# A decoder layer on one core: the odd units of the expert weights issued by GpSimd instead of SyncE

## The chip, the core and the metric

The kernel runs on one NeuronCore of one Trainium2 chip, as one launch. The metric is the device time of the launch in microseconds (us). Of the kernel before, three runs are given with their median.

## The reference, cut to what matters

One step of one decoder layer for 256 prompt tokens and 8 sample tokens, all in float32, width 1024. Behind the attention parts stands a mixture of 32 experts:

```python
logits = xf @ w_router + b_router                 # 264 tokens, 32 experts
top_logit, top_idx = lax.top_k(logits, 4)
gates = jax.nn.softmax(top_logit, axis=-1)
...
gu = xblk @ w_gate_up[e] + b_gate_up[e]           # (1024, 2048) for each expert
g, u = jnp.split(gu, 2, axis=-1)
g = jnp.minimum(g, 7.0); u = jnp.clip(u, -7.0, 7.0)
act = (u + 1.0) * g * jax.nn.sigmoid(1.702 * g)
return act @ w_down[e] + b_down[e]                # (1024, 1024) for each expert
```

Each expert has 8 MB of gate and up weights and 4 MB of down weights (MB here is 1,048,576 bytes), so all 32 hold 384 MB, that is 402.7 million bytes. All of it is read once.

## The kernel before, in words

**Stages.** Projections, convolution, windowed attention, memory attention and the router come first. Their weights and cached keys and values stream through `ring`, 12 slots of 1 MB in SBUF. After that comes the expert stage, which is the longer part.

**Items, units and places.** The experts are taken in pairs (A, B), two pairs to a round, eight rounds. A pair is 24 items of 1 MB: 8 of gate and up for A, 8 for B, 4 of down for A, 4 for B (`item_of`, L523). Two neighbouring items are a unit of 2 MB, so a pair has 12 units, a round 24 (`ROUND // 2`), and all experts 192; this text numbers them 0 to 191. There is room for 16 items, which makes 8 places (`UNITS`), and unit u always goes to place u % 8. `PLACES` (L147) says where a place lies: places 1, 2, 3, 4, 6 and 7 are two neighbouring slots of the ring, place 0 is 16 KB per partition of other memory, and place 5 is two pieces of 8 KB per partition that do not lie side by side. A unit is therefore one DMA of 2 MB with 16 KB for each partition, but at place 5, an odd one, it is two DMAs of 1 MB with 8 KB for each partition (`unit_load`, L631). Place 5 holds units 5, 13, ..., 181, 189.

**Who issues.** All expert weights are issued by SyncE (SP), in order of u, on its one DMA queue. Before it issues unit u, `unit_read` (L648) makes SP wait until TensorE has read unit u - 8, which lay at the same place. The first 8 units are issued late in the attention stages, as the memory for them comes free; the other 16 units of round 0 follow one by one, and a loop (`round_loads`, L661) issues the seven further rounds. A second loop is there for inputs in which an expert has more tokens than 64 slots hold; it is behind an `If` and the profile shows no load of it.

**Who waits.** TensorE takes the items in order. `item_arrived` (L543) waits for the semaphore of the unit's place. `gate_up` (L2114) multiplies the tokens of one expert by 8 items; for A it also scatters the pair before (L2184) between items. `down` (L2156) multiplies by 4 items. Between them stand a turning of the activations (L2153) and the gathering of the next pair's tokens (L2098). The last pair also has L2205, sums that prepare the last layer norm. After the last unit come L2245, the layer norm and the stores of the outputs.

**GpSimd (POOL).** It issues small loads and stores over a queue of its own (the queue called software_dynamic in the profile) and computes little: two subtractions at L797 that the gathering waits for, and two operations on the output rows at the very end (L802, L804). Between L797 and L802 it has nothing to do.

Of the kernel before, what the change touches and what calls it, by code (L numbers as in the profile page):

```python
# [149 lines left out]
def decoder_layer(nc, x_prompt, x_sample, mem_prompt, cache_win_k, cache_win_v, state_conv, cache_mem_k,  # L150
# [4 lines left out]
    with ctx:  # L155
        def sem(name):
            return ctx.enter_context(nc.semaphore(name))
# [333 lines left out]
        def reader_done(eng, n):  # L491

            what, i = STREAM[n]
            if what == "xp":
                eng.wait_ge(s_xT, DC)
            elif what == "mp":
                eng.wait_ge(s_mT, DC)
            elif what == "win":
                piece_used(eng, 2 * i + 1)
            elif what == "wout" and i < 2:  # L500
                eng.wait_ge(s_sd, 1)
            elif what == "wmo" and i < 3:
                eng.wait_ge(s_sd, 2)
            elif what in GROUP0:
                if i % 2 == 0:
                    eng.wait_ge(s_half, GROUP0[what] + i // 2 + 1 - GROUP0["wmv"])
                else:
                    per = 2 if what in ("wmv", "wmk") else 4
                    eng.wait_ge(s_dn, TILE0[what] + per * (i // 2 + 1))
            elif what == "qb":  # L510
                eng.wait_ge(s_kq, 2 * i + 2)
            elif what == "wk":
                eng.wait_ge(s_kr, i + 1)
            elif what == "mqb":
# [66 lines left out]
        down_rows = w_down[0]  # L581
        pos = sample_positions()
        assert pos == list(range(0, 512, 16)) + list(range(512, 896, 4)) + list(range(896, PAST))

        block = ctx.enter_context(nc.Block())

# [3 lines left out]
        def _(sp):  # L590
# [40 lines left out]
            def unit_load(e0, u):  # L631

                k, i = item_of(2 * u)
                e = e0 + k
                if i < 8:
                    src = gate_rows[bass.ds(e, 1), i * P:(i + 2) * P, :].rearrange("a (p s) n -> p (a s) n", s=2)
                else:
                    src = down_rows[bass.ds(e, 1), (i - 8) * 2 * P:(i - 6) * 2 * P, :].rearrange(
                        "a (p s v) n -> p (a s) (v n)", s=2, v=2)
                w, done, first = u % UNITS, unit_landed(u), unit_first(u)  # L640
                if w and first is None:
                    for s in range(2):
                        sp.dma_start(expert_slot(2 * w + s), src[:, s, :]).then_inc(done, 16)
                else:
                    dst = ring[:, first:first + 2, :].rearrange("p a n -> p (a n)") if w else extra_whole
                    sp.dma_start(dst, src.rearrange("p s n -> p (s n)")).then_inc(done, 16)

            def unit_read(k0, u):  # L648

                k, i = item_of(2 * u + 1)  # L650
                k += k0
                if i < 7:
                    sp.wait_ge(e_wu, 7 * k + (i + 1))
                elif i == 7:
                    sp.wait_ge(e_gu, k + 1)
                elif i < 11:
                    sp.wait_ge(e_du, 3 * k + (i - 7))
                else:
                    sp.wait_ge(e_dn, k + 1)

            def round_loads(e0, before):  # L661

                for u in range(ROUND // 2):
                    if u < UNITS:
                        unit_read(before, u + ROUND // 2 - UNITS)
                    else:
                        unit_read(before + 4, u - UNITS)
                    unit_load(e0, u)


            sp.wait_ge(s_av, H + MH)
            sp.wait_ge(s_mst, 32)
            unit_load(0, 0)
            for u in range(1, UNITS):
                at = PLACES[u]
                if at is None:
                    sp.wait_ge(s_sat, 4)
                else:
                    reader_done(sp, NPRE + at - RING)
                    reader_done(sp, NPRE + at + 1 - RING)  # L680
                unit_load(0, u)
            for u in range(UNITS, ROUND // 2):
                unit_read(0, u - UNITS)
                unit_load(0, u)
            with sp.Fori(1, NX // 4) as r:
                round_loads(r * 4, (r - 1) * 4)

            sp.wait_ge(s_nsw, 4)
            rounds = sp.value_load(nswi[0:1, 1:2], min_val=8, max_val=40)
            with sp.If(rounds > NX // 4):  # L690
                with sp.Fori(NX // 4, rounds) as r:
                    round_loads((r % 8) * 4, (r - 1) * 4)
# [16 lines left out]
        def _(pool):  # L709
# [75 lines left out]

            pool.wait_ge(s_kvst, 96)
            pool.dma_start(wr, w_router[0].rearrange("(c p) e -> p c e", p=P)).then_inc(s_late, 16)
            pool.wait_ge(s_dn, 56)
            pool.dma_start(g3[:, 0, :], ln3_g.broadcast_to((P, D))).then_inc(s_g3, 16)
            pool.dma_start(g3[:, 1, :], ln3_b.broadcast_to((P, D))).then_inc(s_g3, 16)  # L790
# [4 lines left out]
            for t in range(2):  # L795
                pool.wait_ge(s_x2b, t + 1)
                nc.gpsimd.tensor_tensor(x3[:, t, 2, :], rest[:, t, :], x3[:, t, 1, :], ALU.subtract).then_inc(s_x3, 1)  # L797

            y1 = yo[:, LORDER[0], :]
            pool.wait_ge(s_g3, 32)  # L800
# [1475 lines left out]
```

## Time and profile before

| | |
|---|---|
| median of 3 runs | 1275.05 us (1274.89 to 1276.47) |
| the profiled execution | 1275.87 us |
| its span in the profile | 1274.1 us, granted TensorE clock 0.995 |
| TensorE busy | 1205.9 us, 95% of the span |
| VectorE, ScalarE, GpSimd busy | 373.0, 201.1, 39.0 us |
| DMA | 485.10 million bytes, mean 381 GB/s |

The span is the time from the first to the last instruction of the program; the profiled execution's own time is 1.77 us more, and lies 0.82 us above the median. A matmul's end is modelled in the profile, so that TensorE can show as busy without being at its peak. GB/s are 10^9 bytes a second.

### The profile page before, as it was taken

To read this page: it belongs to the slowest core of one execution; us is meant where nothing else is said; L and a number is where in the kernel's file an instruction comes from. 1 tells how busy PE (TensorE), PEld (TensorE's weight loads), DVE (VectorE), ACT (ScalarE), POOL (GpSimd) and SP (SyncE) were. 2 spreads that over 40 slices of the span, in tenths; PEclk is the share of its full clock that TensorE was granted. 3 is DMA by queue.
4 is the path that set the end of the run, shared out by engine and by line. 5 is a ranking of instruction groups with operands and counts; after the bars stand their busy time and mean duration, and the time that the engine had idled before them with its cause. 6 is when DMAs were issued, how large, how long until landed. Compare 5 with 4: busy or idle time off the path is not lost.

```text
span 1274.1 us, 16471 instructions
## 1 busy us (share of the span) xinstructions
PE 1205.9 (95%) x6600; PEld 569.8 (45%) x6600; DVE 373.0 (29%) x919; ACT 201.1 (16%) x328; POOL 39.0 (3%) x62
## 2 busy tenths in 40 slices
PE   7999999999999999999989999998989898989896
PEld 6995467876533434344333333232333333233332
DVE  4555735633530221302122021302021211202123
ACT  4443331222301101011010101010101101010101
POOL 2201000100100000000000000000000000000001
PEclk9999999999999999999999999999999999999998
DMA  9984896899499999999999999999999999999993
GB/s 331 292 252 137 264 348 254 333 366 393 165 399 426 429 427 427 428 426 430 426 427 427 427 429 427 427 427 427 426 429 426 428 427 426 430 427 426 426 425 160
DMA packets 62645, 485.10 MB, mean 381 GB/s; under 512 B 6192, under 2 KB 6532, under 8 KB 34352
## 3 DMA queue, kind: packets, MB, share of 16 engines
q1 hardware_dynamic: 58576, 469.36, 90.5%
q0 software_dynamic: 3872, 15.12, 3.7%
q8 instruction: 26, 0.43, 0.1%
q10 hardware_dynamic: 160, 0.10, 0.0%
q14 instruction: 11, 0.09, 0.0%
HBM read 479.40 MB, written 5.17 MB: 380 GB/s over the span
## 4 chain that ended last, share of the span: by engine, by line
PE 62%; DMA 33%; DVE 2%; ACT 1%; issue 1%; SPq 0%; POOL 0%; DVEq 0%; ACTq 0%; POOLq 0%
PE ps L2126 25%; DMA ring<-in_w_gate_up_dram 16%; DMA late<-in_w_gate_up_dram 13%; PE ps L1686 11%; PE ps L2166 6%; PE ps L2184 5%; PE ps L1723 5%; DMA late<-in_w_down_dram 3%; PE ps L2098 1%; PE ps L1867 1%; DMA arena<-in_b_gate_up_dram 1%; PE ps L2153 1%; DMA arena<-in_state_conv_dram 1%; PE ps L2192 1%; PE ps L1889 1%; PE ps L1666 1%
## 5 line engine op out<-in xcount | busy, mean ns | idle before, releaser
L2126 PE MATMUL ps<-ring,arena 128*64 128x512 f32 x1536 | 360.2, 600 | 13.8 <-DMA ring<-in_w_gate_up_dram 13.8
L1583 DVE TENSOR_TENSOR arena<-arena,ps 128x264 f32<-128x264 f32 x128 | 55.2, 431 | 574.7 <-PE ps L2184 574.7
L2126 PEld LDWEIGHTS ps<-ring,arena 128*64 128x64 f32 x1536 | 98.9, 136 | 199.1 <-issue 161.0
L2166 PE MATMUL ps<-ring,arena 128*64 128x512 f32 x768 | 171.6, 596 | 13.5 <-DMA ring<-in_w_down_dram 13.5
L2166 PEld LDWEIGHTS ps<-ring,arena 128*64 128x64 f32 x768 | 53.7, 137 | 118.1 <-issue 104.4
L1004 ACT ACTIVATE arena<-arena 128x512 f32<-128x512 f32 x32 | 20.2, 632 | 471.2 <-DVE arena L1566 471.2
L2184 PE MATMUL ps<-arena 128*128 128x264 f32 x256 | 91.2, 438 | 0.0
L2126 PE MATMUL ps<-late,arena 128*64 128x512 f32 x384 | 90.0, 596 | 0.0
L1686 PE MATMUL ps<-arena,ring 128*128 128x256 f32 x384 | 88.1, 380 | 0.0
L2184 PEld LDWEIGHTS ps<-arena 128*128 128x128 f32 x256 | 38.1, 188 | 103.8 <-issue 103.8
L1723 PE MATMUL ps<-x_split,w_split 128*128 128x264 f32 x384 | 73.7, 293 | 6.7 <-DVE ring_split L1037 6.7
L1686 PEld LDWEIGHTS ps<-arena,ring 128*128 128x128 f32 x384 | 70.8, 189 | 10.9 <-issue 1.8
L1723 PEld LDWEIGHTS ps<-x_split,w_split 128*128 128x128 f32 x384 | 61.6, 195 | 7.9 <-DVE ring_split L1037 7.8
L1686 PE MATMUL ps<-ring,arena 128*128 128x512 f32 x128 | 57.0, 593 | 0.0
L1723 PE MATMUL ps<-x_split,ring_split 128*128 128x264 f32 x192 | 55.8, 290 | 0.0
L2126 PE MATMUL ps<-arena 96*64 96x512 bf16 (+1 forms) x256 | 50.7, 495 | 4.5 <-DMA late<-in_w_gate_up_dram 3.7
L1566 DVE TENSOR_SCALAR arena<-ps 128x512 f32<-128x512 f32 x32 | 22.2, 692 | 111.8 <-PE ps L2126 111.3
L1006 ACT COPY arena<-ps 128x512 f32<-128x512 f32 x32 | 18.8, 587 | 221.1 <-PE ps L2153 221.1
L2098 PE MATMUL ps<-arena 128*128 128x128 bf16 x768 | 52.6, 219 | 1.1 <-issue 1.1
L2098 PEld LDWEIGHTS ps<-arena 128*128 128x128 bf16 x768 | 49.9, 98 | 2.1 <-issue 1.9
L2166 PE MATMUL ps<-late,arena 128*64 128x512 f32 x192 | 44.2, 595 | 6.2 <-DMA late<-in_w_down_dram 6.2
L2126 PEld LDWEIGHTS ps<-late,arena 128*64 128x64 f32 x384 | 25.8, 136 | 45.2 <-issue 42.2
(297 smaller groups left out, 954.7 us busy)
## 6 DMA issues: line engine op xcount, KB each, us to landing
ring<-in_w_gate_up_dram SPq DMA_DIRECT2D x96, 2048.0 KB, 33.8
ring<-in_w_down_dram SPq DMA_DIRECT2D x48, 2048.0 KB, 34.3
late<-in_w_gate_up_dram SPq DMA_DIRECT2D x16, 2048.0 KB, 33.8
arena<-in_w_gate_up_dram SPq DMA_DIRECT2D x16, 1024.0 KB, 31.9
late<-in_w_gate_up_dram SPq DMA_DIRECT2D x16, 1024.0 KB, 34.1
late<-in_w_down_dram SPq DMA_DIRECT2D x8, 2048.0 KB, 35.3
ring<-in_w_in_dram SPq DMA_DIRECT2D x11, 1024.0 KB, 15.5
ring<-in_cache_mem_k_dram SPq DMA_DIRECT2D x8, 1024.0 KB, 6.9
```

The source lines that it names most:

```text
L1004: nc.scalar.activation(sg_, g2, ACT.Sigmoid, scale=1.702).then_inc(e_sig, 1)
L1006: nc.scalar.copy(actT, ps[:, 2, :].rearrange("p (q n) -> p q n", q=4)).then_inc(e_at_out, 1)
L1566: nc.vector.tensor_scalar(g2, ps[:, b, :], 7.0, None, ALU.min).then_inc(e_g2, 1)
L1583: nc.vector.tensor_tensor(xT[:, c, :], xT[:, c, :], ps[:, 2 + c % 2, 0:T], ALU.add).then_inc(e_y_out, 1)
L1666: mm(out, ident, ident.unsqueeze(1).broadcast_to((P, 4, P)), start=True, stop=True)
L1686: ins = mm(out(n), lhs(w, k, kk), rhs(w, k, kk), start=(kk == 0), stop=(kk == 7))
L1723: ins = mm(ps[:, n % 4, 0:T], w[:, cols], x[kk], start=(kk == 0 and m == 0), stop=(kk == 7 and m == 2))
L1867: ins = mm(out, w, halves((vv, b))[:, t, a:z], start=(t == 0), stop=(t == 1))
L2098: mm(out, x3[:, t, k, P * c:P * c + P], Sel[:, t].rearrange("p a s -> p (a s)"), start=(t == 0 and k == 0), stop=False)
L2126: ins = mm(ps[64 * j:64 * j + 64, 6 * a + gu, :], x, w[:, D * gu + 512 * j:D * gu + 512 * j + 512], start=(c < 0), stop=(c == 7), skip_gro ...
L2166: ins = mm(ps[64 * j:64 * j + 64, 4 + half, :], x, w[:, kk, 512 * half:512 * half + 512], start=(m == 0), stop=(m == 7), skip_group_check= ...
L2184: mm(ps[:, 2 + c % 2, 0:T], yb[:, half, P * (c % 4):P * (c % 4) + P], SelT[:, half, :], start=True, stop=True).then_inc(e_y, 1)
```

## The change

The loads are given an issuing engine as a parameter. SP issues the even units, each waiting for the reader of its own place as before; POOL issues the odd units over its own queue, in the same manner. SP's order among the even ones, and POOL's among the odd ones, stay. Each odd place has a semaphore of its own (`landed_odd`), which counts from zero, instead of the ring slot's semaphore; the place at other memory that is even keeps `landed_extra`. Addresses, sizes and shapes of all DMAs stay as they are.

```diff
-        landed_extra = [sem(f"landed_extra{i}") for i in range(2)]
+        landed_extra = sem("landed_extra")
+        landed_odd = [sem(f"landed_odd{i}") for i in range(UNITS // 2)]
...
         def unit_landed(u):
+            if u % 2:
+                return landed_odd[u % UNITS // 2]
             first = unit_first(u)
-            return landed_extra[1 if u % UNITS else 0] if first is None else landed[first]
+            return landed_extra if first is None else landed[first]
...
-            base = 0 if first is None else LBASE[first]
+            base = 0 if first is None or u % 2 else LBASE[first]
...
+        def round_loads(eng, e0, before, odd):
+
+            for u in range(odd, ROUND // 2, 2):
+                if u < UNITS:
+                    unit_read(eng, before, u + ROUND // 2 - UNITS)
+                else:
+                    unit_read(eng, before + 4, u - UNITS)
+                unit_load(eng, e0, u)
...
@@ SyncE @@
-            for u in range(1, UNITS):
+            for u in range(2, UNITS, 2):
...
-            for u in range(UNITS, ROUND // 2):
-                unit_read(0, u - UNITS)
-                unit_load(0, u)
+            for u in range(UNITS, ROUND // 2, 2):
+                unit_read(sp, 0, u - UNITS)
+                unit_load(sp, 0, u)
             with sp.Fori(1, NX // 4) as r:
-                round_loads(r * 4, (r - 1) * 4)
+                round_loads(sp, r * 4, (r - 1) * 4, 0)
...
@@ GpSimd, between the load of w_router (L787) and that of ln3_g (L789) @@
+            for u in range(1, UNITS, 2):
+                at = PLACES[u]
+                if at is None:
+                    pool.wait_ge(s_sat, 4)
+                else:
+                    reader_done(pool, NPRE + at - RING)
+                    reader_done(pool, NPRE + at + 1 - RING)
+                unit_load(pool, 0, u)
...
@@ GpSimd, behind the two subtractions (L797) @@
+            for u in range(UNITS + 1, ROUND // 2, 2):
+                unit_read(pool, 0, u - UNITS)
+                unit_load(pool, 0, u)
+            with pool.Fori(1, NX // 4) as r:
+                round_loads(pool, r * 4, (r - 1) * 4, 1)
```

**On SP, the loads of the first round.** The names in brackets are the semaphores waited for: `s_...` of the attention stages, `e_wu`, `e_gu`, `e_du`, `e_dn` of TensorE's reads of gate and up items (the last one `e_gu`) and of down items (the last one `e_dn`). Before, from unit 6 to unit 15:

```order
L646 DMA ring<-in_w_gate_up_dram 128x4096 [waits s_sd]
L646 DMA ring<-in_w_gate_up_dram 128x4096 [waits s_dn,s_sd]
L646 DMA late<-in_w_down_dram 128x4096 [waits e_wu]
L646 DMA ring<-in_w_down_dram 128x4096 [waits e_wu] x2
L646 DMA ring<-in_w_down_dram 128x4096 [waits e_gu]
L646 DMA ring<-in_w_gate_up_dram 128x4096 [waits e_wu]
L643 DMA arena<-in_w_gate_up_dram 128x2048 [waits e_wu]
L643 DMA late<-in_w_gate_up_dram 128x2048
L646 DMA ring<-in_w_gate_up_dram 128x4096 [waits e_wu]
L646 DMA ring<-in_w_gate_up_dram 128x4096 [waits e_gu]
```

Now, on SP, units 8 to 22:

```order
L603 DMA late<-in_w_down_dram 128x4096 [waits e_wu]
L603 DMA ring<-in_w_down_dram 128x4096 [waits e_wu]
L603 DMA ring<-in_w_gate_up_dram 128x4096 [waits e_wu] x2
L603 DMA late<-in_w_gate_up_dram 128x4096 [waits e_du]
L603 DMA ring<-in_w_gate_up_dram 128x4096 [waits e_du]
L603 DMA ring<-in_w_down_dram 128x4096 [waits e_wu] x2
```

Of the refills, those of the odd places, among them both DMAs of place 5 (L643 before), have left SP, and the wait in front of each has gone with them.

**On POOL, from the router's weights to the second subtraction.** Before:

```order
L787 DMA arena<-in_w_router_dram 128x8x32 [waits s_kvst]
L789 DMA arena<-in_ln_g_dram 128x1024 [waits s_dn]
L790 DMA arena<-in_ln_b_dram 128x1024
L793 DMA arena<-in_b_down_dram 32x1024 [waits s_yz]
L797 ISA
L797 TENSOR_TENSOR arena<-arena 128x1024 [waits s_x2b] x2
```

Now:

```order
L786 DMA arena<-in_w_router_dram 128x8x32 [waits s_kvst]
L603 DMA ring<-in_w_gate_up_dram 128x4096 [waits s_sav] x2
L600 DMA arena<-in_w_gate_up_dram 128x2048 [waits s_sat]
L600 DMA late<-in_w_gate_up_dram 128x2048
L603 DMA ring<-in_w_gate_up_dram 128x4096 [waits s_dn,s_sd]
L796 DMA arena<-in_ln_g_dram 128x1024 [waits s_dn]
L797 DMA arena<-in_ln_b_dram 128x1024
L800 DMA arena<-in_b_down_dram 32x1024 [waits s_yz]
L804 ISA
L804 TENSOR_TENSOR arena<-arena 128x1024 [waits s_x2b] x2
L603 DMA ring<-in_w_down_dram 128x4096 [waits e_wu]
L603 DMA ring<-in_w_down_dram 128x4096 [waits e_gu]
```

Units 1, 3, 5 and 7 now stand ahead of the loads of `ln3_g`, `ln3_b` and `b_down` and of the subtractions; unit 9 and all later odd units stand behind the subtractions.

## Rows read from the trace of the kernel before

**Rows 1.** The page's parts 1 and 2: busy time, and the span in 40 slices.
```profile
PE 1205.9 (95%) x6600; PEld 569.8 (45%) x6600; DVE 373.0 (29%) x919; ACT 201.1 (16%) x328; POOL 39.0 (3%) x62
...
DMA  9984896899499999999999999999999999999993
GB/s 331 292 252 137 264 348 254 333 366 393 165 399 426 429 427 427 428 426 430 426 427 427 427 429 427 427 427 427 426 429 426 428 427 426 430 427 426 426 425 160
```

**Rows 2.** Windows: busy PE, PEld, DVE, ACT, POOL, granted clock, DMA share, GB/s.
```profile
340.00:400.00 60.00, 59.84 (x311) 22.36 (x313) 11.77 (x25) 7.05 (x9) 0.00 (x0) 1.00 0.92 370
400.00:1200.00 800.00, 757.86 (x3942) 279.96 (x3940) 156.94 (x321) 78.78 (x97) 0.00 (x0) 1.00 1.01 427
1240.00:1250.00 10.00, 9.72 (x54) 4.36 (x50) 2.71 (x5) 0.87 (x2) 0.00 (x0) 1.00 1.03 437
```

**Rows 3.** Chain of waits: start, length, engine, what, at the start of four pairs.
```profile
394.26 3.87 PE ps L2126 x20
...
448.17 3.87 PE ps L2126 x20
...
910.11 1.94 PE ps L2126 x8
...
969.02 1.94 PE ps L2126 x8
```

**Rows 4.** Timeline of SP, 280 to 400 us: start, length, line, DMA, count.
```profile
303.11 6.12 SPq L646 DMA_DIRECT2D ring<-in_w_gate_up_dram  x2
344.26 0.33 SPq L646 DMA_DIRECT2D late<-in_w_down_dram  x1
349.29 10.37 SPq L646 DMA_DIRECT2D ring<-in_w_down_dram  x3
```

**Rows 5.** Line L646 from 1219 us on: the issue of unit 191.
```profile
L646 SPq DMA_DIRECT2D ring<-in_w_down_dram x1: 333/333/333, 1219.7 to 1219.7; - x1
...
DMA to landing us min/median/max: 34.3/34.3/34.3
```

**Rows 6.** Timeline of PE in the last pair: start, busy, shape, idle before.
```profile
1204.46 1.94 PE L2126 MATMUL ps<-arena 128*64 128x512 f32 x8 [0.60 <-DMA late<-in_w_gate_up_dram]
...
1210.01 1.94 PE L2126 MATMUL ps<-ring,arena 128*64 128x512 f32 x8 [0.47 <-DMA ring<-in_w_gate_up_dram]
...
1215.03 1.94 PE L2126 MATMUL ps<-ring,arena 128*64 128x512 f32 x8
...
1225.36 3.65 PE L2126 MATMUL ps<-ring,arena 128*64 128x512 f32 x16
...
1251.49 7.09 PE L2166 MATMUL ps<-ring,arena 128*64 128x512 f32 x32
```

**Rows 7.** DMA answer for 309.5 to 312.5 us: packets and queue.
```profile
DMA packets 172, 1.28 MB, mean 426 GB/s; under 512 B 16, under 2 KB 16, under 8 KB 16
```

**Rows 8.** DMA answer for 1150 to 1153 us.
```profile
DMA packets 85, 1.28 MB, mean 426 GB/s; under 512 B 7, under 2 KB 7, under 8 KB 7
```

**Rows 9.** DMA answers for 314 to 319 us and 313.4 to 319.4 us: both queues at work.
```profile
DMA packets 233, 2.14 MB, mean 428 GB/s; under 512 B 23, under 2 KB 23, under 8 KB 124
q1 hardware_dynamic: 120, 1.73, 84.6%
q0 software_dynamic: 113, 0.41, 21.2%
...
DMA packets 287, 2.49 MB, mean 414 GB/s; under 512 B 30, under 2 KB 30, under 8 KB 157
```

**Rows 10.** Timeline of POOL: start, length, what, idle before.
```profile
309.12 0.54 POOL L789 DMA_DIRECT2D arena<-in_ln_g_dram  x1 [69.64 <-PE ps L1686]
...
321.06 0.52 POOL L793 DMA_DIRECT2D arena<-in_b_down_dram  x1 [10.88 <-DVE arena L1454]
328.44 2.27 POOL L797 TENSOR_TENSOR arena<-arena 128x1024 bf16<-128x1024 f32 x1 [6.87 <-ACT arena L988]
```

**Rows 11.** DMA answer for 344 to 345 us: issue of unit 8, us to landing.
```profile
late<-in_w_down_dram SPq DMA_DIRECT2D x1, 2048.0 KB, 7.7
```

**Rows 12.** DMA issues by line: a small load of POOL, us to landing.
```profile
arena<-scratch_self POOLq DMA_DIRECT2D x1, 0.4 KB, 2.2
```

More of the change, by code:

```diff
@@ L583, in decoder_layer, with unit_load, unit_read @@
         assert pos == list(range(0, 512, 16)) + list(range(512, 896, 4)) + list(range(896, PAST))
+        def unit_load(eng, e0, u):
+            k, i = item_of(2 * u)
+            e = e0 + k
+            if i < 8:
+                src = gate_rows[bass.ds(e, 1), i * P:(i + 2) * P, :].rearrange("a (p s) n -> p (a s) n", s=2)
+            else:
+                src = down_rows[bass.ds(e, 1), (i - 8) * 2 * P:(i - 6) * 2 * P, :].rearrange(
+                    "a (p s v) n -> p (a s) (v n)", s=2, v=2)
+            w, done, first = u % UNITS, unit_landed(u), unit_first(u)
+            if w and first is None:
+                for s in range(2):
+                    eng.dma_start(expert_slot(2 * w + s), src[:, s, :]).then_inc(done, 16)
+            else:
+                dst = ring[:, first:first + 2, :].rearrange("p a n -> p (a n)") if w else extra_whole
+                eng.dma_start(dst, src.rearrange("p s n -> p (s n)")).then_inc(done, 16)
+        def unit_read(eng, k0, u):
+            k, i = item_of(2 * u + 1)
+            k += k0
+            if i < 7:
+                eng.wait_ge(e_wu, 7 * k + (i + 1))
+            elif i == 7:
+                eng.wait_ge(e_gu, k + 1)
+            elif i < 11:
+                eng.wait_ge(e_du, 3 * k + (i - 7))
+            else:
+                eng.wait_ge(e_dn, k + 1)
+        def round_loads(eng, e0, before, odd):
+            for u in range(odd, ROUND // 2, 2):
+                if u < UNITS:
+                    unit_read(eng, before, u + ROUND // 2 - UNITS)
+                else:
+                    unit_read(eng, before + 4, u - UNITS)
+                unit_load(eng, e0, u)
         block = ctx.enter_context(nc.Block())
@@ L629, in _ @@
                     sp.dma_start(two, c.rearrange("(k p) n -> p k n", p=P)).then_inc(done, 16)
[L631 to L668, printed above, removed]
@@ L671, in _ @@
             sp.wait_ge(s_av, H + MH)
             sp.wait_ge(s_mst, 32)
-            unit_load(0, 0)
-            for u in range(1, UNITS):
+            unit_load(sp, 0, 0)
+            for u in range(2, UNITS, 2):
                 at = PLACES[u]
[L676 to L680, printed above, removed]
-                unit_load(0, u)
-            for u in range(UNITS, ROUND // 2):
-                unit_read(0, u - UNITS)
-                unit_load(0, u)
+                reader_done(sp, NPRE + at - RING)
+                reader_done(sp, NPRE + at + 1 - RING)
+                unit_load(sp, 0, u)
@@ L685, in _ @@
+            for u in range(UNITS, ROUND // 2, 2):
+                unit_read(sp, 0, u - UNITS)
+                unit_load(sp, 0, u)
             with sp.Fori(1, NX // 4) as r:
-                round_loads(r * 4, (r - 1) * 4)
+                round_loads(sp, r * 4, (r - 1) * 4, 0)
             sp.wait_ge(s_nsw, 4)
@@ L691, in _ @@
                 with sp.Fori(NX // 4, rounds) as r:
-                    round_loads((r % 8) * 4, (r - 1) * 4)
+                    round_loads(sp, (r % 8) * 4, (r - 1) * 4, 0)
             yp = y_prompt[0].rearrange("(k p) n -> p k n", p=P)
@@ L787, in _ @@
             pool.dma_start(wr, w_router[0].rearrange("(c p) e -> p c e", p=P)).then_inc(s_late, 16)
+            for u in range(1, UNITS, 2):
+                at = PLACES[u]
+                if at is None:
+                    pool.wait_ge(s_sat, 4)
+                else:
+                    reader_done(pool, NPRE + at - RING)
+                    reader_done(pool, NPRE + at + 1 - RING)
+                unit_load(pool, 0, u)
             pool.wait_ge(s_dn, 56)
@@ L797, in _ @@
                 nc.gpsimd.tensor_tensor(x3[:, t, 2, :], rest[:, t, :], x3[:, t, 1, :], ALU.subtract).then_inc(s_x3, 1)
+            for u in range(UNITS + 1, ROUND // 2, 2):
[3 more added lines that the diff above has]
+                round_loads(pool, r * 4, (r - 1) * 4, 1)
+            pool.wait_ge(s_nsw, 4)
+            rounds = pool.value_load(nswi[0:1, 1:2], min_val=8, max_val=40)
+            with pool.If(rounds > NX // 4):
+                with pool.Fori(NX // 4, rounds) as r:
+                    round_loads(pool, (r % 8) * 4, (r - 1) * 4, 1)
             y1 = yo[:, LORDER[0], :]
```

## The prediction

> **What bounds the kernel now.** I read the busy times and slices first. TensorE shows 95% busy, which would make it the bound, but from the twelfth slice to the last but one the DMA engines show 9 tenths or more, and from the thirteenth on they move 422 to 430 GB/s almost without change [rows 1]. A window over 400 to 1200 us gives the mean: DMA share 1.01, 427 GB/s; TensorE is busy 757.86 of 800 us there and has room left [rows 2]. At 427 GB/s a unit of 2,097,152 bytes takes 4.91 us, and a pair of 12 units 58.9 us.
>
> Which of the two sets the pace is seen in the chain, by the distance between the starts of pairs. Early it is 448.17 - 394.26 = 53.9 us, late 969.02 - 910.11 = 58.9 us [rows 3]. So TensorE needs 53.9 us for a pair; it starts with 8 units in memory, eats that lead, and then goes at the DMA's 58.9. The expert stage ends when the last bytes come. The first refill, unit 8, is issued at 344.26 [rows 4]; unit 191, the last, is issued at 1219.7 and lands 34.3 us later, at 1254.0 [rows 5]. Between lie 909.7 us for 184 units, and 184 x 4.91 = 903.7 us of that are bytes. A load from issue to landing lasts 34.3 us, seven units' time: as soon as a place is read, its refill is queued behind seven others. So the queue never runs dry, and SP, although it waits for TensorE most of the time, delays nothing.
>
> The last place where TensorE waits for a DMA is in the last pair: 0.60 us before unit 181 (place 5) at 1204.46 and 0.47 us before unit 182 at 1210.01 [rows 6]. From there it works without a gap worth naming, 1274.1 - 1204.46 = 69.6 us to the end of the span. That fits the bytes: when unit 181 has landed, 10 units are still to come, 49.1 us, and 1254.0 - 49.1 = 1204.9. **The end is therefore the landing of the last unit that TensorE has to wait for, plus the work behind it; not the landing of the last byte alone.** In unit order the two come to the same.
>
> **The change, part by part.**
>
> *Bytes and pace.* The DMAs, their sizes and their number are the same: 0 us, as long as the engines take as long over a packet as now. The one stretch in which both queues were at work on large transfers, while POOL loaded the norm's rows beside units 6 and 7, gives 428 GB/s in one window and 414 in one that is 1 us longer [rows 9]. Packets at the edges make up most of such a difference in so short a window, and these packets were small. I take 427 kept, and keep 414 as one end: 903.7 x (427/414 - 1) = 28.4 us more. The other end is 437 GB/s, which the engines showed for 10 us near the end [rows 2]: 903.7 x (1 - 427/437) = 20.7 us less.
>
> *Issue.* SP issues 96 units fewer, POOL 96 more (120 DMAs, since each of the 24 at place 5 is two). POOL's issue shows as 0.54 us against SP's 0.33 [rows 4, 10]. POOL has 50 us and more for each pair and 7 or 8 DMAs to issue in it. What hides the issue is the backlog in front of the engines; where there is none yet, at unit 9 (SP's issue at 349.29), a later start would cost its whole delay. A unit issued by SP with idle engines lands after 7.7 us [rows 11], 2.8 more than its bytes; a small load of POOL lands after 2.2 us [rows 12]. I see no extra latency in that and take 0, with up to 2 us kept in the range.
>
> *The moved issues on POOL.* Units 1, 3, 5 and 7 now stand ahead of the norm's rows, of `b_down` and of the subtractions. SP got to issue units 6 and 7 from 303.11 on, 6.12 us for the two [rows 4], so 7 goes out at about 309; the norm's load stood at 309.12 and is delayed by about 1 us of issuing; `b_down` was issued at 321.06 and the first subtraction ran at 328.44, both after waits of their own [rows 10]. All are still reached in time: 0 us. The odd units from 9 on, which now stand behind the subtractions, cannot be due before the gathering that needs those subtractions. Last, the two operations on the output rows stand behind the odd loads, whose last is issued some 30 us before them: 0 us.
>
> *The order in which units land.* This is the term that counts. Before, units land in the order in which TensorE wants them. Now two queues feed the same 16 engines. How the engines divide themselves can be read where both were busy: in 5 us, 120 packets of the one queue and 113 of the other, with 1.73 and 0.41 MB [rows 9]. Packets alternate one for one, whatever their size. Of what size are they? At place 5, 172 packets less 16 tiny ones carry 1.28 MB, 8.2 KB each [rows 7]; elsewhere 85 less 7 carry as much, 16.4 KB each [rows 8]. So a DMA engine moves a unit in 8 packets, but the unit at place 5 in 16. Of four odd units in a turn through the places, one is at place 5: 3 x 8 + 16 = 40 packets, and beside them go 40 even packets, 5 even units. The evens gain one unit per turn until they can't: an even place is only refilled when it is read, so their lead ends at their four places. After a few of the 23 turns of refills the even units lie ready and TensorE waits for odd ones alone. The engines stay busy, the last byte still lands at 1254.0, but what comes last is different.
>
> I count at unit 181, the last one waited for before. When it lands, the odd units 183, 185, 187, 189 and 191 are still to come. Of the evens, 182, 184 and 186 have landed; 188 could be issued when 180 was read, just before; 190 only after 182 has been read. That is 5 + 2 = 7 units, 34.4 us, so 181 lands at 1254.0 - 34.4 = 1219.6, against 1204.46: **15.1 us later**. Behind it TensorE needs unit 183 after 10.6 us and unit 185 after 20.9 us (1215.03 and 1225.36, less 1204.46) [rows 6]; two units at most go by for each, 9.8 and 19.6 us, so it doesn't wait again. The whole rest moves by 15.1 us. With 188 already landed 6 units are left and it is 20.1 us; with a smaller lead, 8 left, 10.2 us.
>
> *Sum:* 0 + 0 + 0 + 15.1. The span becomes 1289.2, the profiled execution 1291.0, and the median, which lies 0.82 lower, **1290.2 us**.
>
> A rule stands against this: by the Trainium skill (DMA: Bandwidth & Descriptors, Issuing engines are not separate DMA queues) transfers of several issuers run on the same engines and interleave, and spreading them only saves issue time. By that alone the sum is 0 and the time 1275.05. The rows agree that they interleave; which unit comes late because of it, the rule leaves out.
>
> **The rivals.**
>
> *Shared by bytes, not by packets.* Then the evens gain no lead, an even and the next odd unit come side by side, and the waited-for unit is late by at most one unit's time, 4.9 us: 1280.0. Against it speaks the count of packets [rows 9]; for it, that neither side had packets of 16 KB on both queues there. Chance 0.12.
>
> *The order kept.* If the engines took a whole unit from one queue and then one from the other, units would land nearly as before: 1275. The one-for-one count [rows 9] speaks against it. Chance 0.08. The Trainium skill (the same page, Queues, rings and completion order) has the engines drain a packet of typically 9 to 17 descriptors before they turn to the next queue, and this would be that case; the rows count single pieces of 4 to 16 KB in turn, which disagrees.
>
> *The late order, and a slower pace.* Two streams of reads, or POOL's way of feeding the engines, lower the rate. At 420 GB/s it is 903.7 x (427/420 - 1) = 15.1 us more, 1305.3; at 414, 1318.6. For it speaks the 414 [rows 9]. Chance 0.15. The Trainium skill (the same page, Latency and other measured facts) calls two of the engines slower, and guesses at the rings that POOL's transfers use; no row here shows single engines.
>
> *Faster: two queues fill the engines' gaps.* If a second queue lets an engine start its next packet sooner, the pace rises. It decides from 434.3 GB/s on, where 903.7 x (1 - 427/434.3) = 15.2 us pay for the late order. At 437 the time is 1275.05 + 15.1 - 20.7 = 1269.5. For it speaks that 437 was seen [rows 2]; against it, a share of 1.01 at 427 for 800 us, and no gain where both queues worked. Chance 0.08.
>
> **How the numbers follow.** The forecast by itself has 0.57: 1285 to 1295. The range leaves out the faster case, the kept order and the upper part of the slower pace, and begins between 1275 and 1280: 1277 to 1305. Within 0.2% (2.6 us, about what a measurement of this kernel can tell from none) lies the kept order, 0.08; faster is 0.08; slower 0.57 + 0.15 + 0.12 = 0.84.
>
> **What would show it.** In the trace after: POOL's queue with about 200 million bytes more; 427 GB/s over 400 to 1200 us still; the last landing near 1254; waits of TensorE only before odd units, above all place 5, late ones of some us; issue to landing much shorter for SP's units than for POOL's; unit 181 begun near 1220 and 69.6 us from there to the end. The forecast is wrong if TensorE waits for even units as often, if SP's and POOL's loads take equally long to land, or if the rate leaves 427 by more than 1%.

## The result, and the profile after

The changed kernel takes 1288.3 us (median of 4 runs, 1287.44 to 1289.21) against 1274.97 of the kernel before in the same session (4 runs, 1274.35 to 1276.47). The ratio is 1.0103, with a 95% interval of 1.0085 to 1.012: 13.3 us slower, where 15.1 were forecast. The profiled execution took 1288.42 us, 12.5 more than the one of before. Its span is 1286.6 us (also 12.5 more), and its granted TensorE clock 0.976 (0.995 before).

The page of the changed kernel, parts 1 to 3, 5 and 6 (the lines that answer to [rows 1], then the DMA queues with their share of 16 engines, one group of matmuls, and the issues with the median from issue to landing):

```profile
PE 1214.8 (94%) x6600; PEld 575.6 (45%) x6600; DVE 373.1 (29%) x919; ACT 201.1 (16%) x328; POOL 102.7 (8%) x182
...
PEclk9999999999999999999989998999899899989999
...
GB/s 324 291 251 148 261 353 231 368 337 429 153 406 428 426 429 427 428 429 428 427 427 427 427 427 427 430 427 427 428 427 428 428 426 428 428 426 428 427 379 34
...
q1 hardware_dynamic: 41296, 268.03, 52.6%
q0 software_dynamic: 21152, 216.46, 40.6%
...
L2184 PE MATMUL ps<-arena 128*64 128x512 f32 x64 | 24.1, 895 | 33.9 <-DMA late<-in_w_down_dram 33.9
...
ring<-in_w_gate_up_dram SPq DMA_DIRECT2D x48, 2048.0 KB, 13.8
ring<-in_w_gate_up_dram POOLq DMA_DIRECT2D x48, 2048.0 KB, 29.8
ring<-in_w_down_dram POOLq DMA_DIRECT2D x24, 2048.0 KB, 24.8
ring<-in_w_down_dram SPq DMA_DIRECT2D x24, 2048.0 KB, 15.8
```

What to see: the DMA engines run at 427 GB/s as before, until the last slices. The bytes are shared between the queues, but SP's units land after 14 to 16 us and POOL's after 25 to 30. Most of TensorE's time lost sits in one small group, the 64 matmuls on the first item of place 5 when it holds down weights: 33.9 us of waiting, and 895 ns for one matmul where the wide group of the page shows 600. The clock row has five eights in the expert stage, where before only the last slice had one.

Windows of the changed kernel (columns as in [rows 2]: length, busy PE, PEld, DVE, ACT, POOL, granted clock, DMA share, GB/s):

```profile
400.00:1200.00 800.00, 753.14 (x3834) 278.31 (x3834) 157.02 (x321) 76.58 (x94) 54.36 (x103) 0.97 1.01 427
1142.20:1147.00 4.80, 4.78 (x12) 1.49 (x14) 0.00 (x0) 0.00 (x0) 0.00 (x0) 0.50 1.01 430
1142.20:1286.60 144.40, 133.70 (x678) 51.46 (x678) 33.69 (x67) 14.48 (x20) 11.71 (x15) 0.96 0.78 329
```

The same view of the kernel before, from the same matmul to the end:

```profile
1126.00:1274.10 148.10, 132.21 (x678) 50.53 (x678) 33.68 (x67) 14.48 (x20) 4.85 (x2) 0.98 0.87 369
```

Waits of TensorE by the line they stand at: us in total, times, longest. First the changed kernel:

```profile
PE ps L2184 <- DMA late<-in_w_down_dram: 33.9, 5, 7.7
PE ps L2144 <- DMA late<-in_w_gate_up_dram: 7.0, 3, 4.5
```

and the kernel before:

```profile
PE ps L2126 <- DMA ring<-in_w_gate_up_dram: 13.8, 26, 0.6
PE ps L2166 <- DMA ring<-in_w_down_dram: 13.5, 11, 1.4
PE ps L2166 <- DMA late<-in_w_down_dram: 12.3, 10, 1.2
```

Gaps of over 0.4 us before a matmul that a DMA ended, counted from 345 us on, come to 43.2 us in 53 waits before, and to 46.5 us in 11 waits after. The sum of waiting is nearly the same. Before, it came in drops of 0.5 to 1.4 us, about five to a pair; now it comes in lumps of up to 7.7 us. Each of the 11 waits ends 0.04 us after the landing of an odd unit: 33, 37, 57, 69, 93, 109, 115, 117, 141, 157 and 165, eight of them of place 5. The chain of waits of the changed kernel shows them (start, length, what):

```profile
870.03 37.27 DMA late<-in_w_down_dram
...
988.26 34.32 DMA late<-in_w_down_dram
...
1105.83 36.34 DMA late<-in_w_down_dram
...
1159.17 3.87 PE ps L2144 x20
...
1213.08 3.87 PE ps L2144 x20
```

The starts are some 118 us apart, two pairs: this is the unit of place 5 that holds down weights, once per round. The last such load lands at 1142.2. Behind it the chain holds only TensorE, and its pairs start 1213.08 - 1159.17 = 53.9 us apart, TensorE's own pace [rows 3]. Before, it was the DMA's 58.9 until unit 182, the last one waited for.

**Where the 12.5 us come from.** The unit of that last wait is 165 (place 5 again). Timeline of PE, changed kernel, then before (start, busy, shape, idle before):

```profile
1142.22 3.68 PE L2184 MATMUL ps<-arena 128*64 128x512 f32 x8 [7.16 <-DMA late<-in_w_down_dram]
1145.69 2.61 PE L2184 MATMUL ps<-late,arena 128*64 128x512 f32 x8
1148.23 0.75 PE L2171 MATMUL ps<-arena 128*128 128x128 f32 x4
```

```profile
1125.99 1.94 PE L2166 MATMUL ps<-arena 128*64 128x512 f32 x8 [1.23 <-DMA late<-in_w_down_dram]
1127.76 1.89 PE L2166 MATMUL ps<-late,arena 128*64 128x512 f32 x8
```

And the issues of units 165 and 191 in the changed kernel (one line for each DMA: ns to issue, when; us from issue to landing, two DMAs for 165):

```profile
L600 POOL DMA_DIRECT2D late<-in_w_down_dram x1: 527/527/527, 1105.8 to 1105.8; - x1
...
DMA to landing us min/median/max: 29.7/33.0/36.3
...
L603 POOL DMA_DIRECT2D ring<-in_w_down_dram x1: 527/527/527, 1232.7 to 1232.7; - x1
...
DMA to landing us min/median/max: 20.6/20.6/20.6
```

- The last byte lands at 1232.7 + 20.6 = 1253.3, against 1254.0 before [rows 5]. The DMA did its work in the same time.
- Unit 165 is taken up at 1142.22 against 1125.99: +16.2 us. In units: (1253.3 - 1142.2)/4.91 = 22.6 are still to come, where in unit order it is 26. The evens are 3.4 units ahead, and 3.4 x 4.91 = 16.7.
- From there to the end it takes 144.4 us, against 148.1. The waits for a DMA that followed before (seven of 0.47 to 1.24 us, 5.2 together) are gone. The first 16 matmuls take 1148.23 - 1142.22 = 6.0 us where they took 3.6, +2.4: the granted clock is 0.50 for those 4.8 us, its lower level of 1.2 GHz, after a wait of 7.16 us. About -0.9 us is left over, which I did not trace.
- 16.2 - 5.2 + 2.4 - 0.9 = 12.5 us.

### The profile page after: what moved, and what is told of

The parts are those of the page before. It is cut to its first block, busy times and chain, and to the rows that moved or that the text cites. A ratio compares the mean times of both kernels' runs of the same rounds, so it can differ in the third digit from the quotient of the medians.

```text
span 1286.6 us, 16476 instructions
## 1 busy us (share of the span) xinstructions
PE 1214.8 (94%) x6600; PEld 575.6 (45%) x6600; DVE 373.1 (29%) x919; ACT 201.1 (16%) x328; POOL 102.7 (8%) x182
## 3 DMA queue, kind: packets, MB, share of 16 engines
q0 software_dynamic: 21152, 216.46, 40.6%
## 4 chain that ended last, share of the span: by engine, by line
PE 70%; DMA 25%; DVE 2%; issue 1%; ACT 1%; POOL 0%; SPq 0%; POOLq 0%; DVEq 0%; ACTq 0%
PE ps L2144 24%; DMA late<-in_w_down_dram 14%; PE ps L2184 14%; PE ps L1704 11%; DMA late<-in_w_gate_up_dram 7%; PE ps L1741 5%; PE ps L2202 4%; PE ps L2116 3%; DMA ring<-in_w_down_dram 3%; PE ps L2171 1%; PE ps L1885 1%; DMA arena<-in_b_gate_up_dram 1%; DMA arena<-in_state_conv_dram 1%; PE ps L1907 1%; PE ps L1684 1%
## 5 line engine op out<-in xcount | busy, mean ns | idle before, releaser
L2184 PEld LDWEIGHTS ps<-ring,arena 128*64 128x64 f32 x768 | 53.9, 138 | 109.0 <-issue 100.5
L2144 PE MATMUL ps<-late,arena 128*64 128x512 f32 x384 | 90.6, 600 | 0.0
L603 POOL DMA_DIRECT2D ring<-in_w_gate_up_dram x48 | 25.4, 528 | 439.6 <-PE ps L2184 208.7
L2184 PE MATMUL ps<-arena 128*64 128x512 f32 x64 | 24.1, 895 | 33.9 <-DMA late<-in_w_down_dram 33.9
## 6 DMA issues: line engine op xcount, KB each, us to landing
ring<-in_w_gate_up_dram SPq DMA_DIRECT2D x48, 2048.0 KB, 13.8
late<-in_w_down_dram SPq DMA_DIRECT2D x8, 2048.0 KB, 13.8
```

Of the source, the lines that this page charges most:

```text
L603: eng.dma_start(dst, src.rearrange("p s n -> p (s n)")).then_inc(done, 16)
L2144: ins = mm(ps[64 * j:64 * j + 64, 6 * a + gu, :], x, w[:, D * gu + 512 * j:D * gu + 512 * j + 512], start=(c < 0), stop=(c == 7), skip_gro ...
L2184: ins = mm(ps[64 * j:64 * j + 64, 4 + half, :], x, w[:, kk, 512 * half:512 * half + 512], start=(m == 0), stop=(m == 7), skip_group_check= ...
```

## The experiments

In all nine, two tuples say which places each engine loads, and their edits are shown against the changed kernel. In eight of them each place has its own semaphore counting from zero; the halves by both engines keep the semaphores of the kernel before for SP's half and have a new one per place for POOL's.

```diff
...
-            return landed_extra if first is None else landed[first]
+            return landed_place[u % UNITS]
...
-            for u in range(odd, ROUND // 2, 2):
+            for u in [u for u in range(ROUND // 2) if u % UNITS in mine]:
```

Theory A is that of the prediction: engines alternate packet for packet between the queues, so the queue with the smaller packets falls behind, and TensorE waits for its units. The rivals put the loss on POOL's queue or issue, on having two queues at all, or on the semaphores.

### All units issued by POOL

```diff
+OF_SP = ()
+OF_POOL = (0, 1, 2, 3, 4, 5, 6, 7)
```

> All units, even and odd, are issued by POOL on its one queue; SP issues none of them. Theory A (order: two queues are served packet by packet in turn, place 5 has twice the packets, so odd units come late): one queue, units land in order, so 1275 us (1272 to 1278), waits of TensorE about 5 us a pair, every unit about 34 us from issue to landing, 427 GB/s. Rival B (POOL's queue or its way of issuing is itself slower, by issue, by descriptors or by completion): 1288 us or more, with the rate over 400 to 1200 us under 427 GB/s or waits of TensorE before even and odd units alike. Rival C (two queues cost something as such): also 1275.

Measured: 1279.81 us (5 runs, 1278.52 to 1279.87) against 1274.8, ratio 1.004 (1.0025 to 1.0054). The window over the expert stage, one of its waits, and the timeline's last store of the output:

```profile
400.00:1200.00 800.00, 757.40 (x3944) 279.79 (x3941) 156.59 (x320) 79.20 (x97) 99.29 (x188) 1.00 1.01 427
...
SPq L157 <- PEq L157: 4.2, 1, 4.2
...
1270.03 0.34 SPq L708 DMA_DIRECT2D out_dram<-late  x1
```

427 GB/s, and 52 waits of 43.2 us in total, as before. The last store of the output goes out at 1270.03, which is 1.85 us earlier than before (1271.88). So POOL's queue feeds the engines as well as SP's, and one queue keeps the order, whoever owns it. The total is nevertheless 1.8 us above the range that was expected of theory A. In this execution the excess is all behind the last store: 6.2 us from it to the end of the span, against 2.2 before, with SP waiting 4.2 us at the end for the others. That is a cost of its own, taken up in the last section. The 1.85 us are no gain to count on, for this execution (1278.52) is the shortest of the five; of the 5.0 us between the medians, 4.0 stand behind the last store and about 1 us is not located.

### Even units by POOL, odd ones by SP

```diff
+OF_SP = (1, 3, 5, 7)
+OF_POOL = (0, 2, 4, 6)
```

> The odd units on SP, the even ones on POOL. Theory A: the late ones are those that share a queue with place 5, whoever issues them: about 1288 us (1284 to 1292), SP's whole units 25 to 30 us to landing, POOL's about 14, long waits before place 5. Rival B (POOL's queue is slower): the even units on POOL are the late ones, POOL's landings stay the longer ones, and waits stand before even places.

Measured: 1292.0 us, the upper end of what was expected, against 1274.8, ratio 1.0133 (1.0116 to 1.015). Issues over 400 to 1200 us (median from issue to landing), and TensorE's largest wait:

```profile
ring<-in_w_gate_up_dram SPq DMA_DIRECT2D x41, 2048.0 KB, 31.6
...
ring<-in_w_gate_up_dram POOLq DMA_DIRECT2D x41, 2048.0 KB, 14.3
```

```profile
PE ps L2177 <- DMA late<-in_w_down_dram: 28.0, 5, 7.7
```

The picture is turned over: now SP's units land after 31.6 us and POOL's after 14.3, with the rate still 427 GB/s. Late is the queue that has place 5, not a certain engine. This rules out a slow GpSimd queue. The end of the span holds 4.5 us more than before behind the last store, which theory A does not have, so the loss up to that store (1285.34 - 1271.88 = 13.5 us) is close to the changed kernel's (1284.41 - 1271.88 = 12.5).

### Place 0 in two pieces as well: 40 packets on either side

```diff
-            if w and first is None:
+            if first is None:
```

> As the change, but the unit of place 0 (even) is also issued as two DMAs of 1 MB with 8 KB rows. Now 3 x 8 + 16 = 40 packets stand on either side. Theory A: no queue gains a lead, landings of SP and POOL within some 4 us of each other, a waited-for unit late by at most one unit's time of 4.9 us: 1275 to 1280, I say 1279. Rivals B and C: nothing changes against the change, 1288.

Measured: 1282.02 us against 1274.8, ratio 1.0055 (1.0038 to 1.0072). Issues over 400 to 1200 us, and TensorE's largest wait:

```profile
ring<-in_w_gate_up_dram POOLq DMA_DIRECT2D x41, 2048.0 KB, 29.9
...
ring<-in_w_gate_up_dram SPq DMA_DIRECT2D x41, 2048.0 KB, 31.6
```

```profile
PE ps L2177 <- DMA late<-in_w_down_dram: 30.1, 12, 3.5
```

This is the decisive run. Nothing of the two queues is changed; only the packets per turn are evened out (SP had 32, now 40 like POOL). The landing times become equal, the longest wait falls from 7.7 to 3.5 us, and the loss from 13.3 to 7.2 us. The rest is 2.0 us above the range that I expected. The last landing is 1255.3, 1.3 us later, for a reason that the experiment with halves on one queue shows below. The other 5.9 are near one unit's 4.91 us, the price of the rival "shared by bytes": an even and the next odd unit land side by side, so the one that is wanted first has to wait for parts of the second. The trace bears this out at the last long wait, before unit 176:

```profile
1186.17 1.12 PE L2177 MATMUL ps<-late,arena 128*64 128x512 f32 x2 [2.87 <-DMA late<-in_w_down_dram]
```

Unit 176 lands at 1186.12 and unit 177 at 1186.29, and (1255.3 - 1186.1)/4.91 = 14.1 units are still to come, where in unit order it is 15. Before, TensorE took unit 176 up at 1179.92, 6.2 us earlier: 0.9 unit is 4.4 us of that, the later last landing 1.3.

One rival is left by all of these runs. A DMA is 8 pieces for each engine whatever its rows, so if the engines took a whole DMA from each queue in turn, the shares would be the same, 5 DMAs to 4 in the change and 5 to 5 here. The trace of the changed kernel tells the two apart. A piece of 16 KB takes an engine 16384/(427000/16) = 0.61 us, and eight of them 4.9. Two windows of 0.6 us, 1120.3 to 1120.9 and 1120.9 to 1121.5, where the engines happened to be in step and both queues had large pieces waiting:

```profile
q0 software_dynamic: 15, 0.25, 96.3%
q1 hardware_dynamic: 1, 0.02, 6.4%
...
q1 hardware_dynamic: 15, 0.25, 96.0%
q0 software_dynamic: 1, 0.02, 6.4%
```

The engines serve POOL's queue (q0) for one piece and then SP's (q1) for one. It is pieces that alternate, not DMAs, and units 176 and 177, landing 0.17 us apart, say the same.

### Every unit in halves, one by each engine

```diff
+            s = half_of[id(eng)]
+            eng.dma_start(expert_slot(2 * (u % UNITS) + s), src[:, s, :]).then_inc(unit_landed(u, s), 16)
```

Each half is 128 rows of 8 KB; SP issues the first item of each unit and POOL the second.

> Every unit is issued as two DMAs of 1 MB with 8 KB rows, the first item by SP and the second by POOL, each with its own semaphore. Both queues are at work all the time, with equal packets and in the order of need. Theory A: 1275 us, at most 5 us more for the smaller packets (426 instead of 427 GB/s is 2 us). Rival C (two queues at once cost something as such): 1285 or more. Rival B: POOL's halves land clearly later than SP's, and TensorE waits before second items.

Measured: 1288.47 us against 1274.8, ratio 1.0104 (1.0087 to 1.012). Window and issues over 400 to 1200 us:

```profile
400.00:1200.00 800.00, 748.55 (x3848) 272.93 (x3842) 157.05 (x321) 76.61 (x94) 86.94 (x164) 1.00 1.01 422
...
ring<-in_w_gate_up_dram SPq DMA_DIRECT2D x81, 1024.0 KB, 35.0
ring<-in_w_gate_up_dram POOLq DMA_DIRECT2D x81, 1024.0 KB, 34.6
```

The order is what the edit was to give: the two halves of a unit land within 0.2 us of each other, no wait is long, the clock is at 1.00. But the rate is 422 GB/s, not 427, and the last byte lands at 1266.4, 12.4 us later than before. By the number alone this is what was expected of the rival that two queues cost something as such. I had allowed about 2 us for this, because 3 us of 8 KB packets showed the same 426 GB/s as 16 KB ones [rows 7, 8]. So the experiment could not tell what order alone costs, and asked for the next one.

### The same halves, all issued by SP

```diff
+OF_SP = (0, 1, 2, 3, 4, 5, 6, 7)
+OF_POOL = ()
...
+            for s in range(2):
+                eng.dma_start(expert_slot(2 * w + s), src[:, s, :]).then_inc(done, 16)
```

> SP alone issues every unit, as two DMAs of 1 MB with 8 KB rows on its one queue; POOL issues none. It tells apart why the halves on two queues took 1288.5 us at 422 GB/s. If the 8 KB packets lower the rate (theory A): 422 GB/s here too, last landing near 1266, 1287 us (1285 to 1290). If two queues at once lower it (rival C): 426 to 427 GB/s and 1275 to 1277 us.

Measured: 1286.04 us (1285.21 to 1287.63) against 1274.25, ratio 1.0097 (1.008 to 1.0113). The window:

```profile
400.00:1200.00 800.00, 749.61 (x3879) 275.12 (x3878) 157.03 (x321) 77.15 (x95) 0.00 (x0) 1.00 1.01 422
```

422 GB/s with one queue too, and the last landing at 1264.2. The lower rate comes with the 8 KB packets, not with the second queue: (427/422 - 1) x 903.7 = 10.7 us. Of the run before, only 1283.54 - 1281.19 = 2.4 us at the last store are due to its second queue. With the order kept, two queues cost little. (The two profiled executions lie 4.4 us apart, the medians 2.4, and 2.1 of those stand behind the last store.) The halves also double the number of DMAs, each with a closing piece of a few bytes for every engine: 2934 pieces under 512 B in this window before, 5146 here. No run separates that from the size of the rows. Place 0 in two pieces adds an eighth of the units at 8 KB, against seven eighths more here: 10.2/7 = 1.5 us by this, and 1.3 were seen.

### Place 7 in two pieces as well: 48 odd packets beside 32

```diff
-            if w and first is None:
+            if w in (5, 7):
```

> As the change, but the units of place 7 (odd) are also two DMAs with 8 KB rows: 2 x 8 + 2 x 16 = 48 odd packets in a turn against 32 even ones, so the evens could gain two units a turn instead of one. Theory A: the lead is bounded by the even places, so it stays what it is, and the time is that of the change plus 1 to 2 us for the smaller packets in one place of eight: 1288 to 1292. A theory in which the loss grows with the imbalance itself would give twice the loss, 1300.

Measured: 1291.7 us against 1274.25, ratio 1.0135 (1.0119 to 1.0152). Issues over 400 to 1200 us:

```profile
ring<-in_w_gate_up_dram SPq DMA_DIRECT2D x41, 2048.0 KB, 12.8
ring<-in_w_gate_up_dram POOLq DMA_DIRECT2D x26, 2048.0 KB, 30.2
```

The surplus of odd packets per turn goes from 8 to 16, yet the loss only from 13.3 to 17.5 us, inside the expected 1288 to 1292. SP's 12.8 us to landing hardly differ from the 13.8 of the changed kernel. So the lead of the even units is near its end already with the small surplus, as it would be if their four places bound it. It is not quite at its end: TensorE waits for unit 181 here,

```profile
1219.66 3.01 PE L2137 MATMUL ps<-arena 128*64 128x512 f32 x8 [2.95 <-DMA late<-in_w_gate_up_dram]
```

and at its landing (1254.7 - 1219.6)/4.91 = 7.1 units are still to come, against 7.9 in the changed kernel. The last landing is 1.4 us later too.

### Place 5 moved from POOL to SP

```diff
+OF_SP = (0, 2, 4, 5, 6)
+OF_POOL = (1, 3, 7)
```

> SP issues places 0, 2, 4, 5 and 6, POOL places 1, 3 and 7. In a turn SP's queue has 4 x 8 + 16 = 48 packets, POOL's 24. Theory A: now POOL's units come early (landing in about 12 us) and SP's late (over 30 us), with the waits of TensorE before units of SP, even ones and place 5: 1283 to 1292. Rival B (POOL's queue is the slower): POOL's units stay the late ones.

Measured: 1294.12 us (1292.89 to 1296.81) against 1274.25, ratio 1.0159 (1.0141 to 1.0178). Issues over 400 to 1200 us, then TensorE's largest wait:

```profile
ring<-in_w_gate_up_dram SPq DMA_DIRECT2D x41, 2048.0 KB, 27.8
ring<-in_w_gate_up_dram POOLq DMA_DIRECT2D x40, 2048.0 KB, 13.9
```

```profile
PE ps L2137 <- DMA ring<-in_w_gate_up_dram: 38.6, 12, 4.7
```

With 48 packets per turn on SP and 24 on POOL, SP's units come late and POOL's early, and TensorE waits for gate and up units in the ring that SP brings. The time is 2.1 us above the range that I had given to theory A; behind the last store stand 7.1 us, 4.9 more than before, which the theory does not have. Up to that store the loss is 1285.35 - 1271.88 = 13.5 us.

### The semaphores alone

```diff
+OF_SP = (0, 1, 2, 3, 4, 5, 6, 7)
+OF_POOL = ()
```

> SP alone issues all units in order as before; only the semaphores change, one for each place counting from zero. All theories: no change, 1275 us (1273 to 1277). If the ending, after the last store, is longer, that part of the all-POOL kernel's loss does not belong to POOL's issuing.

Measured: 1274.66 us (10 runs) against 1274.25 (13 runs), ratio 0.9999 (0.9989 to 1.0008). Counting per place costs nothing, and the end behind the last store stays at 2.2 us, so the longer end with all loads on POOL does not come from the semaphores.

### Only place 7 issued by POOL

```diff
+OF_SP = (0, 1, 2, 3, 4, 5, 6)
+OF_POOL = (7,)
```

> POOL issues place 7 alone, one unit in eight, SP all others. POOL's unit shares the engines packet by packet with SP's, so it lands in some 10 us instead of 34 and passes up to six units that are needed before it. Theory A: each of those is late by at most this one unit's 4.9 us, POOL then has nothing queued until the next turn: 1276 to 1281 us, I say 1279. If any use of POOL's queue in this stage brought the whole loss of the change, it would be 1288.

Measured: 1281.41 us (5 runs, 1280.69 to 1281.53) against 1274.76, ratio 1.0045 (1.0029 to 1.0061). Issues over 400 to 1200 us:

```profile
ring<-in_w_gate_up_dram POOLq DMA_DIRECT2D x14, 2048.0 KB, 14.1
...
ring<-in_w_down_dram SPq DMA_DIRECT2D x34, 2048.0 KB, 32.6
```

One place of eight on the second queue: it lands early every time (14.1 us against 32.6), and that alone delays the other seven. The last store is 1275.63 - 1271.88 = 3.8 us later, near one unit's 4.91. With four places ahead it was 12.5. The whole is 0.4 us above the expected 1276 to 1281, with 1.9 us more than before behind the last store. On these two points the loss grows with the number of places whose units can lie ready too early.

### The runs side by side

The last store leaves out what happens behind it. Each row is one profiled execution, and these lie up to 1.8 us from the median of their kernel; the kernel before and that with the semaphores alone, both in unit order, are 0.8 us apart. Differences of a microsecond or two between rows mean nothing by themselves.

| kernel | last landing | last store issued | from there to the end |
|---|---|---|---|
| before | 1254.0 | 1271.88 | 2.2 |
| the change | 1253.3 | 1284.41 | 2.2 |
| the semaphores alone | 1253.1 | 1271.07 | 2.2 |
| all by POOL | 1252.1 | 1270.03 | 6.2 |
| even by POOL, odd by SP | 1252.3 | 1285.34 | 6.7 |
| 40 packets on either side | 1255.3 | 1278.47 | 2.2 |
| halves, both engines | 1266.4 | 1283.54 | 4.4 |
| halves, SP alone | 1264.2 | 1281.19 | 2.2 |
| 48 odd packets beside 32 | 1254.7 | 1288.17 | 2.2 |
| place 5 on SP | 1254.4 | 1285.35 | 7.1 |
| place 7 alone on POOL | 1252.8 | 1275.63 | 4.1 |

In all kernels that keep 427 GB/s the last landing stays within 2 us of 1254.0, while the last store moves by up to 16.3 us. There the end follows the order of landing, not the last byte.

No version beats the kernel before. It is bound by the DMA from the twelfth slice on, and none of the runs raised the rate. Not tried were larger rows than 16 KB, and place 5 in one piece, which needs another layout of the memory; from the halves, where seven eighths of the units more in 8 KB packets cost 10.2 us, one eighth fewer could bring some 1.5 us.

## Why the prediction was right, and where it was not

**Bytes and pace, 0 us:** right. 427 GB/s over 400 to 1200 us, the last landing 0.7 us earlier. The bounds of 414 and 437 were not needed: with both queues at work for 800 us, nothing of the 414 in one window of [rows 9] is left. POOL's queue carried 216.46 million bytes against 15.12 before, 201 more.

**Issue, and the moved issues on POOL, 0 us:** right. POOL issues a DMA in 0.53 us, the norm's load goes out at 309.32 (309.12 before), and the first subtraction runs at 327.88, 0.56 us earlier than before. With every load on POOL the last store is not later than before either.

**The order of landing, +15.1 us:** the mechanism holds, and TensorE waits before odd units alone. The swap, the evened packets, and place 5 on SP each move the lateness to where alternation packet for packet puts it; evening the packets out removes 6.1 of 13.3 us. The size was over by 1.8 us in the median. The step that failed is the count at unit 181, "Of the evens, 182, 184 and 186 have landed". Unit 186 was issued only at 1209.8, and when 181 landed, at 1214.7, 7.9 units were left and not 7. So it came 10.3 us late, near the bound of 10.2 that the text kept for 8 units left. Nor was 181 waited for: it had landed 2.8 us before TensorE began it, at 1217.52. The last wait had moved forward to unit 165, the down weights of place 5. There the lead was 3.4 units, +16.2 us. The prediction took the last unit waited for before as the one after. But once the waits come in lumps, each leaves TensorE some us behind the loads, and at 53.9 us for a pair against the DMA's 58.9 it makes up only 5.0 us per pair: from unit 165 on it did not catch up in the 111 us that the DMA had left. It was close: in the swap and in the kernel with 48 odd packets TensorE waited for unit 181 as well, 2.96 us until 1216.85 and 2.95 us until 1219.66, with some 7 units still to come, as the prediction had counted. So which unit is the last one waited for is not settled by the mechanism, but by a few microseconds of TensorE's own lateness.

That 15.1 is near 13.3 is in part luck. The forecast took a lead of 3 units at unit 181; measured, it was 2.1 there and 3.4 at unit 165, where it counted.

**"No further wait, 69.6 us to the end":** right as a statement, for the wrong unit. From unit 181's start it took 1286.6 - 1217.52 = 69.1 us. From unit 165 the rest is 3.7 us shorter than before, since the 5.2 us of small waits vanish; the slow clock gives back 2.4 of that. The two terms that I didn't have, -5.2 and +2.4, partly cancel.

**The rivals.** *The order kept* is ruled out: the swap and the evened packets show the lateness on the side with more pieces, and units that lie side by side land 0.17 us apart. By the Trainium skill (DMA: Bandwidth & Descriptors, Queues, rings and completion order) an engine drains a whole packet of typically 9 to 17 descriptors before it turns. (A packet of the profile is one such piece, not a group of them.) That would keep the 8 pieces of a unit for each engine together; this case's trace disagrees, with 15 pieces of one queue and 1 of the other in one window of 0.6 us, and the reverse in the next. *Shared by bytes* is ruled out for the change, but it describes what is left when the packets are even, 7.2 us. *A slower pace by a second queue* is ruled out at 427 GB/s in every run with whole units. *Filling gaps* likewise. Of the same page's rule on issuers (Issuing engines are not separate DMA queues) these runs agree that the transfers interleave on the same engines; that a second issuer "will only save the time on the sequencer" left out the 13.3 us that the interleaving cost here.

**What I had misread:** the counts of [rows 9], 120 packets and 113 in 5 us, did not show that single packets alternate: one DMA of each queue is 8 x 16 = 128 large packets, so whole DMAs in turn would have given about the same. The statement was right, but only the windows of 0.6 us show it. And from 3 us of 8 KB packets [rows 7] I took the packet's size to cost nothing. Over the whole stage it is 427 against 422 GB/s, and the last landing is 10 to 12 us later. In the prediction this touched nothing, since the sizes stayed; in the expectation for the halves it was wrong.

## What to carry to other kernels

When a stream of weights is bound by the DMA engines and eaten in order, its order of landing can be worth as much as its rate: here a second queue added no bandwidth, and whatever it brought early delayed what was wanted first, by 3.8 us with one place that could run ahead and by 12.5 with four, where a unit takes 4.91. Two queues shared the engines packet for packet, so the queue with smaller rows fell behind; before splitting a stream, count the packets on each side, not the bytes. And when looking for the end, count the units still to come at each unit that TensorE may wait for, not only at the one that was last before.

## What the runs showed of the hardware that I had not expected

- The engines alternated between two queues by single pieces, shown for 16 KB: 15 and 1 in one window of 0.6 us, 1 and 15 in the next.
- Rows of 8 KB (and twice the DMAs) against 16 KB, the engines busy all the time: 422 against 427 GB/s, with one queue as with two. A window of 3 us was too short to show it.
- After the long waits TensorE's granted clock was at its lower level: 0.50 over 1142.2 to 1147.0 after 7.16 us without work. In the changed kernel 72 matmul records are 850 ns or longer, in the kernel before none. Whether a little other work on TensorE during such a wait would keep the clock up was not tried.
- GpSimd's queue kept 427 GB/s with all 402.7 million bytes on it, at 0.53 us for an issue against SP's 0.33.
- In five kernels (all by POOL, the swap, the halves by both, place 5 on SP, place 7 alone on POOL) the program ended 4.1 to 7.1 us after its last store, against 2.2 in the others. In the trace of the first, GpSimd's closing drain ends 8.4 us after its last operation, and SP waits for it. The changed kernel and two others with half of the loads on POOL don't show it. What sets it stays open.
